# Differential attention in a long kernel: queries and keys of the second heads by seven products of halves, and values and norm of the first heads one step sooner

## The chip, the cores and the metric

One Trainium2 chip, one of its cores. The metric is the time of one execution of the whole program in microseconds (us) on the device; the program before the change takes 1809.34 us (median of three runs, 1808.73 to 1809.43).

## The reference, cut to what matters

The program computes two blocks: a Mamba-2 mixer, a mixture of experts (MoE), a differential attention, a second MoE, and then a second block of two more layers. The change touches the differential attention alone. There x is 256 tokens by 1024 features (in the kernel: xT, features on the partitions), and

```python
q, k, v = split(x @ w_qkv)          # each 256 x 1024; 8 heads, each of two parts of 64
q, k = rope(q), rope(k)             # on 16 of each 64 columns
p1, p2 = softmax(causal(q1 k1^T / 8)), softmax(causal(q2 k2^T / 8))
o = (p1 - lambda * p2) @ v          # per head, 128 wide
o = rms_norm(o) * subln * (1 - lambda_init)
mix = o @ w_o
```

The heads are worked on in two halves ("hg" 0 and 1) of four heads, that is 512 columns of q, k and v each.

## The kernel before, in words

Five in-order instruction streams, one for each engine, are written out by hand; they meet through semaphores (`wait_ge`, `then_inc`). What one function issues on TensorE has its counterparts on ScalarE (copies out of PSUM, exponentials), VectorE (largest scores, shares, rope, norm) and GpSimd (the reciprocal root of the norm, line 3174). `tensor_attention`, `scalar_attention` and `vector_attention` call these parts in a fixed order.

The parts that matter:

- `tensor_qkv(hg, w, t)`: one product of 128 tokens (t) with 512 columns (w: 0 queries, 1 keys, 2 values), eight float32 matmuls 128x512 over the 1024 features. Each float32 matmul stands as two records in the profile, so a product has 16 records (line 212). `scalar_qkv` copies its result (line 1928).
- `tensor_turn_qk` (line 1094) transposes queries or keys after `vector_rope` (lines 2705 to 2711); `scalar_turned_qk` copies them to SBUF (line 1933).
- `tensor_scores(hd)` lays the mask (line 1107) and adds the scores of a head (line 1114). VectorE takes the largest scores (lines 2723, 2725), ScalarE the exponentials (lines 1943, 1945), VectorE the shares (lines 2730 to 2738), and `tensor_turn_p(hd)` transposes them (line 1125), ScalarE copies (line 1950), `tensor_values(hd)` multiplies with the values (lines 1136 to 1138), ScalarE copies and squares (lines 1955 to 1958).
- `vector_subln_var` (line 2786), GpSimd, and `vector_subln` (lines 2791, 2793) do the norm of two heads; `tensor_subln` transposes the result (line 1147), `scalar_subln` copies it (line 1963), and `tensor_attn_out` multiplies with w_o.

Between the scores of a head and the transposition of its shares TensorE is given other work: for the heads 0 to 3 the five products of the second half's queries, keys and values, for head 4 the second half of the product (1, 2, 1), that is the values of the last 128 tokens, and for the heads 5 to 7 pieces of the output projection.

PSUM banks are handed out in turn (`Banks`): who takes a bank waits for what its last user signals. The weights pass through a ring of 8 slots of 2 MB (and a ninth place, xl). `Ring.add` gives each load the slot that has rested longest and the signal that frees it; SyncE issues all loads in order, each after that signal. The first expert weights of the second MoE are loaded while the attention runs. A MoE takes pairs of experts: gate and up products (line 876), down products (line 911), rows gathered (line 810) and spread (line 928).

Of the kernel before, what the change touches and what calls it, by code (L numbers as in the profile page):

```python
# [150 lines left out]
def build(nc, A, out):  # L151
    ctx = ExitStack()
    with ctx:
# [55 lines left out]
        def project(e, bout, lhs, rhs, ks, start=True, stop=True):  # L209
# [62 lines left out]
        QKV = [(0, w, t) for t in range(2) for w in range(3)] + [(1, 2, 0)] + [  # L272
            (1, w, t) for w in range(2) for t in range(2)] + [(1, 2, 1)]
        QKV_LOADS = [(0, 0), (0, 1), (0, 2), (1, 2), (1, 0), (1, 1)]
        qkv_mm, qkv_in = Sig(sem("qkv_mm"), QKV), Sig(sem("qkv_in"), QKV)
        roped = sig("roped", range(2), range(2))
        TQK = [(0, 0), (0, 1), (1, 0), (1, 1)]
# [34 lines left out]
        tu_mm, tu_in = Sig(sem("tu_mm"), TU), Sig(sem("tu_in"), TU)  # L312
        PAIRED = ((0, 0), (1, 0), (0, 1), (1, 1))
        es_mm = Sig(mm_seg.sem, [(u, *x) for u in range(4) for x in PAIRED + ((0, 2),)] + [
            (u, j, t) for u in range(4, 8) for j in range(2) for t in range(2 if j else 3)], mm_seg)
# [17 lines left out]
        oc_in, sq_in, b_in, y_in = then(gained, G8, range(2)), then(xd_in, G8), then(dec_d, G8), then(dec_in, G8)  # L333
        oo_in = Sig(yv_in.sem, [x[0:3] for x in OUT], yv_in)
        og_in, lr_in, lt_in = then(zs_in, G8, range(2)), then(mx_in, G8, G8), then(Bl_in, G8)
        la_in, rt_in, ix_in = then(dec_e, G8), then(S0_in, G8), then(y_rs, G8)


# [54 lines left out]
        ring_moe(0)  # L393
        assert ring.before(*PARTED[:1], 0, *PARTED[1:]) == gate_mm(0, 1, 0)
        for hg, w in QKV_LOADS:
            ring.add(("qkv", hg, w), 1, qkv_mm(hg, w, 1), NSLOT - 1)

        ring.add(("ao", 0), 1, ao_mm(0, 1, 1), NSLOT - 1)
        ring.add(("ao", 1), 1, ao_mm(1, 1, 1), NSLOT - 1)
# [104 lines left out]
        oT = area(big, 0, (8, 256))  # L504
        qT = [area(big, 2048, (4, 256)), area(big, 3072, (4, 256))]
        kT = [area(ring_t[:, NSLOT - 1, :], i * 1024, (4, 256)) for i in range(2)]

        m = Arena(small, 704)
        m(32)
# [562 lines left out]
        def tensor_qkv(e, hg, w, t, ks=range(8)):  # L1072
# [94 lines left out]
        def tensor_attention(e):  # L1167
            for t in range(2):
                if t == 0:
                    tensor_warm(e, row_b[0], 12)  # L1170
                for n in range(2):
                    e.wait_ge(*ln_out("f0", t, n))
                    tensor_turn(e, "f0", t, n, ps[4 * t + n])
                if t == 0:
                    for n in range(2):
                        e.wait_ge(*xT_in("f0", 0, n))
                        tensor_qkv(e, 0, 0, 0, range(4 * n, 4 * n + 4))
            tensor_qkv(e, 0, 1, 0)
            tensor_qkv(e, 0, 2, 0)
            e.wait_ge(*lp_in(0))  # L1180
            e.matmul(ps[7][:, 0:2], ones[:, :], lp, start=True, stop=True).then_inc(*lam_mm.up(0))
            ab.gone[id(ps[7])] = lam_e(0)
            e.wait_ge(*xT_in("f0", 1, 1))
            for w in range(3):
                tensor_qkv(e, 0, w, 1)
            tensor_qkv(e, 1, 2, 0)
            tensor_turn_qk(e, 0, 0)
            tensor_turn_qk(e, 0, 1)
            tensor_scores(e, 0)
            tensor_scores(e, 1)  # L1190
            tensor_qkv(e, 1, 0, 0)
            tensor_turn_p(e, 0)
            tensor_qkv(e, 1, 0, 1)
            tensor_values(e, 0)
            for hd in (1, 2):
                tensor_scores(e, hd + 1)
                tensor_turn_p(e, hd)
                tensor_qkv(e, 1, 1, hd - 1)
                tensor_values(e, hd)
            tensor_turn_p(e, 3)  # L1200
            tensor_qkv(e, 1, 2, 1, range(4))
            tensor_turn_qk(e, 1, 0)
# [24 lines left out]
            tensor_attn_out(e, 1, 1, 1)  # L1227
# [738 lines left out]
        def scalar_attention(e):  # L1966
# [17 lines left out]
            scalar_qkv(e, 1, 2, 0)  # L1984
            scalar_turned_qk(e, 0, 0)
            scalar_turned_qk(e, 0, 1)
            scalar_scores(e, 0)
            scalar_scores(e, 1)
            scalar_qkv(e, 1, 0, 0)
            scalar_turned_p(e, 0)  # L1990
            scalar_qkv(e, 1, 0, 1)
            scalar_values(e, 0)
            for hd in (1, 2):
                scalar_scores(e, hd + 1)
                scalar_turned_p(e, hd)
                scalar_qkv(e, 1, 1, hd - 1)
                scalar_values(e, hd)
            scalar_turned_p(e, 3)
            scalar_turned_qk(e, 1, 0)
            scalar_turned_qk(e, 1, 1)  # L2000
# [695 lines left out]
        def vector_rope(e, hg, w):  # L2696
# [4 lines left out]
            e.wait_ge(*qkv_in(hg, w, 1))  # L2701
            e.wait_ge(*trig(1))
            if hg or w:
                e.wait_ge(*(roped(hg, 0) if w else roped(0, 1)))
# [4 lines left out]
            e.wait_ge(*vs())  # L2709
            e.tensor_tensor(r1, u[0], u[1], ALU.subtract).then_inc(*vs.up())  # L2710
            e.tensor_tensor(r2, u[2], u[3], ALU.add).then_inc(*roped.up(hg, w))

        def vector_scores(e, hd):
            vector_largest_score(e, hd)
# [26 lines left out]
        def vector_attention(e):  # L2741
# [763 lines left out]
```

## Time and profile before

| | |
|---|---|
| median of three runs | 1809.34 us (1808.73 to 1809.43) |
| the profiled execution, its own time | 1808.5 us |
| span of its trace | 1806.7 us |
| TensorE busy | 1785.8 us, 99% |
| VectorE busy | 721.7 us, 40% |
| ScalarE busy | 448.5 us, 25% |
| granted clock of TensorE | 1.00 of full speed |

The span is the time from the first to the last instruction. A share of busy time is an average over stages that have different limits. An engine's idle time costs nothing as long as the engine is not the one that is waited for.

### The profile page before, as it was taken

To read this page: it belongs to the slowest core of one execution; us is meant where nothing else is said; L and a number is where in the kernel's file an instruction comes from. 1 tells how busy PE (TensorE), PEld (TensorE's weight loads), DVE (VectorE), ACT (ScalarE), POOL (GpSimd) and SP (SyncE) were. 2 spreads that over 40 slices of the span, in tenths; PEclk is the share of its full clock that TensorE was granted. 3 is DMA by queue.
4 is the path that set the end of the run, shared out by engine and by line. 5 is a ranking of instruction groups with operands and counts; after the bars stand their busy time and mean duration, and the time that the engine had idled before them with its cause. 6 is when DMAs were issued, how large, how long until landed. Compare 5 with 4: busy or idle time off the path is not lost.

```text
span 1806.7 us, 21260 instructions
## 1 busy us (share of the span) xinstructions
PE 1785.8 (99%) x8612; PEld 983.8 (54%) x8647; DVE 721.7 (40%) x1667; ACT 448.5 (25%) x958; POOL 70.9 (4%) x66
## 2 busy tenths in 40 slices
PE   9999999999999999999999999999999999999999
PEld 8888754443443333455444344343366767568874
DVE  3566754212221213045421221221345566244675
ACT  2332312111111101143211111110134534217780
POOL 0000000000000000000000000000011110001110
PEclk9999999999999999999999999999999999999999
DMA  9723469999999999708999999999932332041520
GB/s 387 306 76 146 186 254 404 426 427 427 427 428 427 427 428 425 315 0 349 359 424 428 427 428 426 428 427 427 425 158 94 140 122 112 7 181 47 238 89 23
DMA packets 41684, 527.41 MB, mean 292 GB/s; under 512 B 4784, under 2 KB 5456, under 8 KB 8560
## 3 DMA queue, kind: packets, MB, share of 16 engines
q1 hardware_dynamic: 39056, 516.70, 68.8%
q10 hardware_dynamic: 2528, 9.31, 1.3%
q8 instruction: 71, 1.16, 0.3%
q14 instruction: 29, 0.24, 0.0%
HBM read 524.91 MB, written 1.08 MB: 291 GB/s over the span
## 4 chain that ended last, share of the span: by engine, by line
PE 87%; DMA 9%; DVE 2%; SPq 1%; issue 0%; ACT 0%; POOL 0%; DVEq 0%; ACTq 0%
PE ps L212 32%; PE ps L876 20%; PE ps L911 10%; DMA ring<-in_wu 6%; PE ps L810 4%; PE ps L928 3%; DMA ring<-in_w_lat 2%; PE ps L715 2%; PE ps L1698 2%; PE ps L1666 2%; PE ps L1234 1%; DMA big<-in_w_z0dt 1%; PE ps L679 1%; PE ps L1713 1%; PE ps L883 1%; PE ps L1446 1%
## 5 line engine op out<-in xcount | busy, mean ns | idle before, releaser
L876 PE MATMUL ps<-ring,work 128*64 128x512 f32 x1856 | 408.9, 593 | 5.5 <-DMA ring<-in_wu 5.1
L212 PE MATMUL ps<-xl,ring 128*128 128x256 f32 (+3 forms) x1344 | 291.6, 375 | 0.6 <-DMA ring<-in_w_x 0.6
L876 PEld LDWEIGHTS ps<-ring,work 128*64 128x64 f32 x1856 | 131.6, 137 | 269.9 <-issue 251.0
L212 PEld LDWEIGHTS ps<-xl,ring 128*128 128x128 f32 x1344 | 243.7, 190 | 39.8 <-issue 2.7
L911 PE MATMUL ps<-ring,work 128*64 128x512 f32 x816 | 181.5, 594 | 0.1
L212 PE MATMUL ps<-ring,xl 128*128 128x256 f32 (+1 forms) x576 | 176.0, 463 | 0.2 <-ACT xl L1783 0.2
L2643 DVE TENSOR_TENSOR work<-work,ps 128x512 f32<-128x512 f32 x32 | 22.0, 687 | 360.6 <-PE ps L876 340.9
L212 PEld LDWEIGHTS ps<-ring,xl 128*128 128x128 f32 x576 | 108.3, 190 | 59.3 <-issue 49.9
L911 PEld LDWEIGHTS ps<-ring,work 128*64 128x64 f32 x816 | 56.2, 137 | 100.3 <-issue 98.7
L3174 POOL TENSOR_TENSOR small<-small,halves 128x1 f32<-128x1 f32 (+4 forms) x42 | 45.7, 1089 | 1546.3 <-DVE small L2445 935.8
L2604 DVE SCALAR_TENSOR_TENSOR work<-ps,small,big 128x512 f32<-128x512 f32 x60 | 45.0, 750 | 135.8 <-ACT big L1914 135.8
L1899 ACT COPY work<-ps 128x512 f32<-128x512 f32 x32 | 18.8, 586 | 305.5 <-PE ps L883 305.5
L1914 ACT ACTIVATE big<-ps,small 128x512 bf16<-128x512 f32 x60 | 41.2, 687 | 182.7 <-PE ps L911 182.7
L212 PE MATMUL ps<-ring,big 128*128 128x512 f32 x192 | 86.2, 595 | 0.2 <-ACT big L1963 0.2
L810 PE MATMUL ps<-work,big 128*128 128x256 bf16 x672 | 78.0, 273 | 0.0
L928 PE MATMUL ps<-big,work 128*128 128x512 bf16 x270 | 69.4, 379 | 4.8 <-issue 4.8
L810 PEld LDWEIGHTS ps<-work,big 128*128 128x128 bf16 x672 | 65.3, 98 | 12.1 <-issue 4.9
L1895 ACT ACTIVATE work<-ps 128x512 f32<-128x512 f32 x32 | 19.1, 597 | 180.8 <-PE ps L876 180.7
L2613 DVE COPY work<-ps 128x512 f32<-128x512 f32 x32 | 22.1, 691 | 97.8 <-PE ps L810 97.1
L212 PEld LDWEIGHTS ps<-ring,big 128*128 128x128 f32 x192 | 34.9, 190 | 39.5 <-issue 39.3
L928 PEld LDWEIGHTS ps<-big,work 128*128 128x128 bf16 x300 | 26.7, 98 | 52.0 <-issue 26.0
L212 PE MATMUL ps<-ring,work 128*128 128x512 f32 (+2 forms) x144 | 50.6, 501 | 0.0
(476 smaller groups left out, 1958.3 us busy)
## 6 DMA issues: line engine op xcount, KB each, us to landing
ring<-in_wg SPq DMA_DIRECT2D x62, 2048.0 KB, 20.2
ring<-in_wu SPq DMA_DIRECT2D x52, 2048.0 KB, 21.4
ring<-in_wd SPq DMA_DIRECT2D x48, 2048.0 KB, 21.9
xl<-in_wd SPq DMA_DIRECT2D x10, 2048.0 KB, 23.2
xl<-in_wu SPq DMA_DIRECT2D x9, 2048.0 KB, 18.4
ring<-in_w_odd SPq DMA_DIRECT2D x8, 2048.0 KB, 7.5
ring<-in_w_xz SPq DMA_DIRECT2D x7, 2048.0 KB, 23.1
ring<-in_w_qkv SPq DMA_DIRECT2D x6, 2048.0 KB, 36.0
```

Of the source, the lines that this page charges most:

```text
L212: i = e.matmul(bout, lhs(k), rhs(k), start=start and k == ks[0], stop=stop and k == ks[-1])
L715: last = e.matmul(oacc[name][:, :], lhs[:, m, :], rhs[:, m, :], start=m == 0 and name in ("p1", "p5", "p2"), stop=m == 6, skip_group_check ...
L810: last = e.matmul(o, hb[:, j, t, c:c + 128], Sb[:, s // 2 % 2, t, :], start=t + j == 0, stop=t + j == 3)
L876: last = e.matmul(b[64 * j:64 * j + 64, :], x[:, 4 * a + k, 64 * j:64 * j + 64], w[k // 2][:, 2 * (k % 2) + j, :], start=a + k == 0, stop= ...
L911: last = e.matmul(b[64 * j:64 * j + 64, :], hT[:, f, 64 * j:64 * j + 64], w[:, j, :], start=f == 0, stop=f == 3)
L928: last = e.matmul(macc[t][n][:, :], SWT[:, p % 2, t * 128:(t + 1) * 128], ypart(j, n), start=p + j == 0, stop=False)
L1666: e.matmul(b[:, c0:272], wl[:, ki, r, (2 * cb + j) % 8, :], xc[cb % 2][:, j, c0:272], start=True, stop=True).then_inc(*lr_mm.up(cb, i))
L1698: last = e.matmul(eb["oo", OB[name]][:, :], lhs[:, k, :], w, start=first and k == 0, stop=k == 5, skip_group_check=True)
L1914: e.activation(ypart(0, n), row_b[n][:, :], ACT.Copy, scale=wsl[:, p % 2:p % 2 + 1]).then_inc(*yh.up(l, p, n))
L2604: e.scalar_tensor_tensor(out=hs, in0=row_b[n][:, :], scalar=wsl[:, p % 2:p % 2 + 1], in1=ypart(0, n), op0=ALU.mult, op1=ALU.subtract).then ...
L2613: e.tensor_copy(gathered(s, 0), gat_b(s)[0][:, :].rearrange("p (k n) -> p k n", k=4 if s < 2 else 2)).then_inc(*xg0.up(l, s))
L3174: e.tensor_tensor(x, x, n[0:x.shape[0]], ALU.pow).then_inc(*done)
```

## The change

Queries and keys of the second half of the heads were four products (two halves of the tokens, queries or keys), each over all features, thirty-two matmuls. They are now computed as a 2 by 2 by 2 block product (token halves, feature halves, queries and keys) with seven products of halves instead of eight: p1 to p7, four matmuls each. For this VectorE forms four sums of x (128x512 each), four sums of the weights (128x2048 each), and ScalarE copies partial results out while VectorE adds others to them. A further ring slot, "qksum", holds the sums. Rope of the second half takes the keys first. The second product of values (1, 2, 1) is finished before the scores of head 4 where its second half came after them; the values of head 3 come before the transpositions of the second half's keys and queries where they came after; and VectorE's norm of the first heads comes ahead of head 4's largest scores.

```diff
-        for hg, w in QKV_LOADS: ring.add(("qkv", hg, w), 1, qkv_mm(hg, w, 1), NSLOT - 1)
+            ring.add(("qkv", hg, w), 1, qkv_mm(hg, w, 1) if hg == 0 or w == 2 else qk_mm("p7" if w else "p4"), NSLOT - 1)
+        ring.add(("qksum",), 0, qk_mm("p7"), NSLOT - 1)
...
+        def tensor_qk_mix(e, name):
+            lhs, rhs = {
+                "p1": (xa(0, 0), wqk(0, 0)), "p5": (xsum[0], qksum), "p2": (xa(0, 1), wqk(1, 0)), "p6": (xsum[1], wqk(0, 0)),
+                "p3": (xsum[3], wqk(1, 1)), "p7": (xsum[2], wqk(0, 1)), "p4": (xa(1, 1), wqk(1, 0))}[name]
...   (waits: p5 on t1; p6 on t2 and r11; p3 on r22; p7 on r12; p4 on t4)
+            for k in range(4):
+                last = e.matmul(ab["qk", bank][:, :], lhs[:, k, :], rhs[:, k, :], start=first and k == 0, stop=k == 3,
+                                skip_group_check=True)
...
@@ tensor_attention
             tensor_qkv(e, 1, 2, 0)
+            tensor_qk_mix(e, "p1")
             tensor_turn_qk(e, 0, 0)
             tensor_turn_qk(e, 0, 1)
             tensor_scores(e, 0)
             tensor_scores(e, 1)
-            tensor_qkv(e, 1, 0, 0)
+            tensor_qk_mix(e, "p5")
+            tensor_qk_mix(e, "p2")
             tensor_turn_p(e, 0)
-            tensor_qkv(e, 1, 0, 1)
+            tensor_qk_mix(e, "p6")
+            tensor_qk_mix(e, "p3")
             tensor_values(e, 0)
-            for hd in (1, 2):
-                tensor_scores(e, hd + 1)
-                tensor_turn_p(e, hd)
-                tensor_qkv(e, 1, 1, hd - 1)
-                tensor_values(e, hd)
+            tensor_scores(e, 2)
+            tensor_turn_p(e, 1)
+            tensor_qk_mix(e, "p7")
+            tensor_qk_mix(e, "p4")
+            tensor_values(e, 1)
+            tensor_scores(e, 3)
+            tensor_turn_p(e, 2)
+            tensor_qkv(e, 1, 2, 1, range(4))
+            tensor_values(e, 2)
             tensor_turn_p(e, 3)
-            tensor_qkv(e, 1, 2, 1, range(4))
+            tensor_qkv(e, 1, 2, 1, range(4, 8))
+            tensor_values(e, 3)
+            tensor_turn_qk(e, 1, 1)
             tensor_turn_qk(e, 1, 0)
-            tensor_turn_qk(e, 1, 1)
-            tensor_values(e, 3)
             tensor_scores(e, 4)
-            tensor_qkv(e, 1, 2, 1, range(4, 8))
             tensor_subln(e, 0, 0)
             tensor_subln(e, 0, 1)
@@ scalar_attention (after the copies for heads 0 to 2, with r11, r22, r12, r21 in them)
             scalar_turned_p(e, 3)
-            scalar_turned_qk(e, 1, 0)
+            scalar_values(e, 3)
+            scalar_qkv(e, 1, 2, 1)
             scalar_turned_qk(e, 1, 1)
-            scalar_values(e, 3)
+            scalar_turned_qk(e, 1, 0)
             scalar_scores(e, 4)
-            scalar_qkv(e, 1, 2, 1)
+        def vector_qk_sums(e):
...   (s1 to s4 of x, then t1 and t3 of the weights, then t2, which waits for p1)
+        def vector_qk_add(e, name, done, copied, bank, x):
+            e.wait_ge(*qk_mm(done))
+            e.wait_ge(*qk_copied(copied))
+            e.tensor_tensor(x, x, ab["qk", bank][:, :], ALU.add).then_inc(*qk_mix.up(name))
@@ vector_attention
             vector_rope(e, 0, 1)
+            vector_qk_sums(e)
             for hd in (0, 1):
                 vector_scores(e, hd)
+            e.wait_ge(*qk_mm("p2"))
+            e.wait_ge(*qk_mix("t2"))
+            e.tensor_tensor(wqk(1, 0), wqk(1, 0), wqk(0, 0), ALU.subtract).then_inc(*qk_mix.up("t4"))
+            vector_qk_add(e, "c11", "p2", "r11", "c", qs[:, 0, :])
             vector_scores(e, 2)
+            vector_qk_add(e, "c12", "p3", "r12", "f", ks_[:, 0, :])
+            vector_qk_add(e, "c22", "p7", "r21", "a", ks_[:, 1, :])
+            vector_rope(e, 1, 1)
+            vector_scores(e, 3)
+            vector_qk_add(e, "c21", "p4", "r21", "e", qs[:, 1, :])
             vector_rope(e, 1, 0)
-            vector_scores(e, 3)
-            vector_rope(e, 1, 1)
             vector_subln_var(e, 0, 0)
             vector_subln_var(e, 0, 1)
-            vector_largest_score(e, 4)
             vector_subln(e, 0, 0)
             vector_subln(e, 0, 1)
+            vector_largest_score(e, 4)
             vector_shares(e, 4)
```

## Rows read from the trace of the kernel before

**Rows 1.** The page: span; busy time of the engine.

```profile
span 1806.7 us, 21260 instructions
PE 1785.8 (99%) x8612; PEld 983.8 (54%) x8647; DVE 721.7 (40%) x1667; ACT 448.5 (25%) x958; POOL 70.9 (4%) x66
```

**Rows 2.** Waits of TensorE, 760 to 852 us: instruction, releaser, us, times, longest.

```profile
PE ps L212 <- ACT big L1963: 0.2, 1, 0.2
```

**Rows 3.** Timeline of TensorE: start, us, line, tiles, records [idle before].

```profile
736.29 27.71 PE L212 MATMUL ps<-ring,xl 128*128 128x512 f32 x64
763.84 1.91 PE L1094 MATMUL ps<-cF,work 128*128 128x128 f32 x16
...
769.01 7.13 PE L212 MATMUL ps<-ring,xl 128*128 128x512 f32 x16
...
802.23 0.49 PE L1125 MATMUL ps<-cF,work 128*128 128x128 f32 x3
802.56 3.60 PE L212 MATMUL ps<-ring,xl 128*128 128x512 f32 x8
806.00 1.91 PE L1094 MATMUL ps<-cF,work 128*128 128x128 f32 x16
807.74 0.39 PE L1136 MATMUL ps<-work 128*128 128x128 f32 x2
...
808.41 0.49 PE L1107 MATMUL ps<-cB 128*128 128x384 bf16 x2
808.83 0.93 PE L1114 MATMUL ps<-ring,big 64*128 64x128 f32 x8
809.69 3.70 PE L212 MATMUL ps<-ring,xl 128*128 128x512 f32 x8
813.23 1.04 PE L1147 MATMUL ps<-cF,work 128*128 128x128 f32 x8
814.10 0.49 PE L1107 MATMUL ps<-cB 128*128 128x384 bf16 x2
...
815.37 0.55 PE L1125 MATMUL ps<-cF,work 128*128 128x128 f32 x3
```

**Rows 4.** Timeline of VectorE.

```profile
767.82 1.15 DVE L2723 TENSOR_REDUCE small<-ps 128x1 f32<-128x128 f32 x4 [15.47 <-PE ps L1114]
...
809.79 1.15 DVE L2723 TENSOR_REDUCE small<-ps 128x1 f32<-128x128 f32 x4
...
814.38 0.48 DVE L2738 SCALAR_TENSOR_TENSOR work<-work,small 128x256 f32<-128x256 f32 x1
```

**Rows 5.** Timeline of ScalarE.

```profile
806.63 1.07 ACT L1933 COPY big<-ps 128x512 f32<-128x512 f32 x2 [2.78 <-PE ps L1094]
807.59 1.09 ACT L1933 COPY ring<-ps 128x512 f32<-128x512 f32 x2
808.61 0.37 ACT L1955 COPY work<-ps 128x256 f32<-128x256 f32 x1
```

**Rows 6.** Groups by line and form on VectorE: count, us in all, mean ns.

```profile
L2671 DVE TENSOR_TENSOR work<-h,big 128x2048 f32<-128x2048 f32 x2 | 4.6, 2284 | 0.0
```

**Rows 7.** SyncE's queue: landing of the loads of in_w_qkv, then issues by start.

```profile
DMA to landing us min/median/max: 31.8/36.0/44.4
...
708.04 0.33 SPq L3232 DMA_DIRECT2D ring<-in_w_qkv  x1
...
757.16 56.58 SPq L3232 DMA_DIRECT2D ring<-in_wu  x2
...
851.06 0.33 SPq L3232 DMA_DIRECT2D ring<-in_wd  x1
```

**Rows 8.** Windows: stretch, length, busy PE, PEld, DVE, ACT, POOL, clock, DMA, GB/s.

```profile
790.00:810.00 20.00, 20.00 (x91) 11.45 (x90) 6.49 (x28) 8.67 (x31) 1.08 (x2) 1.00 0.00 1
840.00:850.00 10.00, 10.00 (x27) 4.62 (x26) 6.23 (x12) 0.69 (x1) 0.99 (x1) 1.00 0.70 298
1300.00:1304.00 4.00, 2.56 (x19) 0.47 (x17) 2.86 (x5) 1.39 (x4) 0.54 (x1) 1.00 1.01 426
```

More of the change, by code:

```diff
@@ L271, in build @@
         lp_in, lam_mm, lam_e = (sig(n, range(1)) for n in ("lp_in", "lam_mm", "lam_e"))
-        QKV = [(0, w, t) for t in range(2) for w in range(3)] + [(1, 2, 0)] + [
-            (1, w, t) for w in range(2) for t in range(2)] + [(1, 2, 1)]
+        QKV = [(0, w, t) for t in range(2) for w in range(3)] + [(1, 2, 0), (1, 2, 1)]
+        qk_mm = then(mm_seg, ("p1", "p5", "p2", "p6", "p3", "p7", "p4"))
+        qk_copied = then(zs_in, ("r11", "r22", "r12", "r21"))
+        qk_mix = then(xd_in, ("s1", "s2", "s3", "s4", "t1", "t3", "t2", "t4", "c11", "c12", "c22", "c21"))
         QKV_LOADS = [(0, 0), (0, 1), (0, 2), (1, 2), (1, 0), (1, 1)]
         qkv_mm, qkv_in = Sig(sem("qkv_mm"), QKV), Sig(sem("qkv_in"), QKV)
-        roped = sig("roped", range(2), range(2))
-        TQK = [(0, 0), (0, 1), (1, 0), (1, 1)]
+        TQK = [(0, 0), (0, 1), (1, 1), (1, 0)]
+        roped = Sig(sem("roped"), TQK)
         qkT_mm = Sig(sem("qkT_mm"), [k + (i,) for k in TQK for i in range(2)])
@@ L314, in build @@
         es_mm = Sig(mm_seg.sem, [(u, *x) for u in range(4) for x in PAIRED + ((0, 2),)] + [
-            (u, j, t) for u in range(4, 8) for j in range(2) for t in range(2 if j else 3)], mm_seg)
+            (u, j, t) for u in range(4, 8) for j in range(2) for t in range(2 if j else 3)], qk_mm)
         es_exp = then(nega_e, U8, range(2), range(3))
@@ L332, in build @@
         odd_mix = then(mix, ("t1a", "t1", "t3", "s1", "s3", "r11", "s2", "t2", "r22", "s4", "t4", "r12", "r21", "r2b"))
-        oc_in, sq_in, b_in, y_in = then(gained, G8, range(2)), then(xd_in, G8), then(dec_d, G8), then(dec_in, G8)
+        oc_in, sq_in, b_in, y_in = then(gained, G8, range(2)), then(qk_mix, G8), then(dec_d, G8), then(dec_in, G8)
         oo_in = Sig(yv_in.sem, [x[0:3] for x in OUT], yv_in)
-        og_in, lr_in, lt_in = then(zs_in, G8, range(2)), then(mx_in, G8, G8), then(Bl_in, G8)
+        og_in, lr_in, lt_in = then(qk_copied, G8, range(2)), then(mx_in, G8, G8), then(Bl_in, G8)
         la_in, rt_in, ix_in = then(dec_e, G8), then(S0_in, G8), then(y_rs, G8)
@@ L395, in build @@
         for hg, w in QKV_LOADS:
-            ring.add(("qkv", hg, w), 1, qkv_mm(hg, w, 1), NSLOT - 1)
+            ring.add(("qkv", hg, w), 1, qkv_mm(hg, w, 1) if hg == 0 or w == 2 else qk_mm("p7" if w else "p4"), NSLOT - 1)
+        ring.add(("qksum",), 0, qk_mm("p7"), NSLOT - 1)
         ring.add(("ao", 0), 1, ao_mm(0, 1, 1), NSLOT - 1)
@@ L506, in build, with xa, wqk @@
         kT = [area(ring_t[:, NSLOT - 1, :], i * 1024, (4, 256)) for i in range(2)]
+        xsum = [area(ring.view("qksum"), 512 * i, (4, 128)) for i in range(4)]
+        qksum = area(ring.view("qksum"), 2048, (4, 512))
+        def xa(t, hf):
+            return xT[:, hf:8:2, t * 128:(t + 1) * 128]
+        def wqk(hf, n):
+            return kview(8, 512)(ring.view("qkv", 1, n))[:, hf:8:2, :]
         m = Arena(small, 704)
@@ L1083, in tensor_qkv @@
                 last.then_inc(*qkv_mm.up(hg, w, t))
+        def tensor_qk_mix(e, name):
+            lhs, rhs = {
+                "p1": (xa(0, 0), wqk(0, 0)), "p5": (xsum[0], qksum), "p2": (xa(0, 1), wqk(1, 0)), "p6": (xsum[1], wqk(0, 0)),
+                "p3": (xsum[3], wqk(1, 1)), "p7": (xsum[2], wqk(0, 1)), "p4": (xa(1, 1), wqk(1, 0))}[name]
+            bank = {"p1": "a", "p6": "a", "p7": "a", "p5": "f", "p3": "f", "p2": "c", "p4": "e"}[name]
+            first = name in ("p1", "p5", "p2", "p4")
+            if first:
+                last_read = {"f": "c12", "c": "c11", "e": "c21"}
+                b, gone = ab.hold(("qk", "a")) if bank == "a" else ab.take(("qk", bank), qk_mix(last_read[bank]))
+                if gone:
+                    e.wait_ge(*gone)
+            if name == "p1":
+                e.wait_ge(*ring("qkv", 1, 0))
+            elif name == "p5":
+                e.wait_ge(*qk_mix("t1"))
+            elif name == "p6":
+                e.wait_ge(*qk_mix("t2"))
+                e.wait_ge(*qk_copied("r11"))
+            elif name == "p3":
+                e.wait_ge(*qk_copied("r22"))
+            elif name == "p7":
+                e.wait_ge(*qk_copied("r12"))
+            elif name == "p4":
+                e.wait_ge(*qk_mix("t4"))
+            for k in range(4):
+                last = e.matmul(ab["qk", bank][:, :], lhs[:, k, :], rhs[:, k, :], start=first and k == 0, stop=k == 3,
+                                skip_group_check=True)
+            last.then_inc(*qk_mm.up(name))
+            if name == "p7":
+                ab.give(ab["qk", "a"], qk_mix("c22"))
         def tensor_turn_qk(e, hg, w):
@@ L1928, in scalar_qkv, with scalar_qk_copy @@
             e.copy((qs, ks_, vs_[hg])[w][:, t, :], ab["qkv", hg, w, t][:, :]).then_inc(*qkv_in.up(hg, w, t))
+        def scalar_qk_copy(e, name, done, bank, to):
+            e.wait_ge(*qk_mm(done))
+            e.copy(to, ab["qk", bank][:, :]).then_inc(*qk_copied.up(name))
         def scalar_turned_qk(e, hg, w):
@@ L1986, in scalar_attention @@
             scalar_turned_qk(e, 0, 1)
+            scalar_qk_copy(e, "r11", "p1", "a", qs[:, 0, :])
             scalar_scores(e, 0)
             scalar_scores(e, 1)
-            scalar_qkv(e, 1, 0, 0)
+            scalar_qk_copy(e, "r22", "p5", "f", ks_[:, 1, :])
             scalar_turned_p(e, 0)
-            scalar_qkv(e, 1, 0, 1)
+            scalar_qk_copy(e, "r12", "p6", "a", ks_[:, 0, :])
             scalar_values(e, 0)
[L1993 to L1997, printed above, removed]
+            scalar_scores(e, 2)
+            scalar_turned_p(e, 1)
+            scalar_qk_copy(e, "r21", "p7", "a", qs[:, 1, :])
+            scalar_values(e, 1)
+            scalar_scores(e, 3)
+            scalar_turned_p(e, 2)
+            scalar_values(e, 2)
             scalar_turned_p(e, 3)
+            scalar_values(e, 3)
+            scalar_qkv(e, 1, 2, 1)
+            scalar_turned_qk(e, 1, 1)
             scalar_turned_qk(e, 1, 0)
-            scalar_turned_qk(e, 1, 1)
-            scalar_values(e, 3)
             scalar_scores(e, 4)
-            scalar_qkv(e, 1, 2, 1)
             scalar_subln(e, 0, 0)
@@ L2700, in vector_rope @@
             u = [x.rearrange("p t (c d) -> p t c d", c=8) for x in u4]
-            e.wait_ge(*qkv_in(hg, w, 1))
+            if hg:
+                e.wait_ge(*qk_mix("c22" if w else "c21"))
+            else:
+                e.wait_ge(*qkv_in(hg, w, 1))
             e.wait_ge(*trig(1))
             if hg or w:
-                e.wait_ge(*(roped(hg, 0) if w else roped(0, 1)))
+                e.wait_ge(*((roped(0, 1) if w else roped(1, 1)) if hg else roped(0, 0)))
             e.tensor_tensor(u[0], r1, cb_, ALU.mult).then_inc(*vs.up())
@@ L2711, in vector_rope @@
             e.tensor_tensor(r2, u[2], u[3], ALU.add).then_inc(*roped.up(hg, w))
+        def vector_qk_sums(e):
+            e.wait_ge(*xT_in("f0", 1, 1))
+            e.wait_ge(*ring.before("qksum"))
+            e.tensor_tensor(xsum[0], xa(1, 0), xa(1, 1), ALU.add).then_inc(*qk_mix.up("s1"))
+            e.wait_ge(*qk_mix("s1"))
+            e.tensor_tensor(xsum[1], xsum[0], xa(0, 0), ALU.subtract).then_inc(*qk_mix.up("s2"))
+            e.tensor_tensor(xsum[2], xa(0, 0), xa(1, 0), ALU.subtract).then_inc(*qk_mix.up("s3"))
+            e.wait_ge(*qk_mix("s2"))
+            e.tensor_tensor(xsum[3], xa(0, 1), xsum[1], ALU.subtract).then_inc(*qk_mix.up("s4"))
+            e.wait_ge(*ring("qkv", 1, 0))
+            e.wait_ge(*ring("qkv", 1, 1))
+            e.tensor_tensor(qksum, wqk(0, 1), wqk(0, 0), ALU.subtract).then_inc(*qk_mix.up("t1"))
+            e.wait_ge(*qk_mix("t1"))
+            e.tensor_tensor(wqk(0, 1), wqk(1, 1), wqk(0, 1), ALU.subtract).then_inc(*qk_mix.up("t3"))
+            e.wait_ge(*qk_mix("t3"))
+            e.wait_ge(*qk_mm("p1"))
+            e.tensor_tensor(wqk(0, 0), wqk(0, 1), wqk(0, 0), ALU.add).then_inc(*qk_mix.up("t2"))
+        def vector_qk_add(e, name, done, copied, bank, x):
+            e.wait_ge(*qk_mm(done))
+            e.wait_ge(*qk_copied(copied))
+            e.tensor_tensor(x, x, ab["qk", bank][:, :], ALU.add).then_inc(*qk_mix.up(name))
         def vector_scores(e, hd):
@@ L2761, in vector_attention @@
             vector_rope(e, 0, 1)
+            vector_qk_sums(e)
             for hd in (0, 1):
                 vector_scores(e, hd)
+            e.wait_ge(*qk_mm("p2"))
+            e.wait_ge(*qk_mix("t2"))
+            e.tensor_tensor(wqk(1, 0), wqk(1, 0), wqk(0, 0), ALU.subtract).then_inc(*qk_mix.up("t4"))
+            vector_qk_add(e, "c11", "p2", "r11", "c", qs[:, 0, :])
             vector_scores(e, 2)
+            vector_qk_add(e, "c12", "p3", "r12", "f", ks_[:, 0, :])
[3 more added lines that the diff above has]
+            vector_qk_add(e, "c21", "p4", "r21", "e", qs[:, 1, :])
             vector_rope(e, 1, 0)
-            vector_scores(e, 3)
-            vector_rope(e, 1, 1)
             vector_subln_var(e, 0, 0)
             vector_subln_var(e, 0, 1)
-            vector_largest_score(e, 4)
             vector_subln(e, 0, 0)
             vector_subln(e, 0, 1)
+            vector_largest_score(e, 4)
             vector_shares(e, 4)
```

## The prediction

> **What bounds the kernel now.** I read the page first: TensorE is busy 1785.8 us of a span of 1806.7 [rows 1]. Then its waits in the attention: between 760 and 852 us it waits 0.2 us in all [rows 2]. So in this stretch every microsecond taken from TensorE's list comes off the end, and every microsecond for which its next instruction is not ready is added. Therefore the third view, the timeline of TensorE there [rows 3], together with those of VectorE and ScalarE [rows 4, 5]: each result that TensorE uses is made by a chain through those two, and what counts is how much work TensorE has in hand meanwhile. Last, the DMA side [rows 7, 8], since the second MoE behind the attention is fed from it.
>
> **Lengths of TensorE's pieces**, from start to start [rows 3]: four products take 763.84 - 736.29 = 27.55 us, so 6.89 each; a half product (four matmuls, 8 records) 806.00 - 802.56 = 3.44; both turns of queries and keys 807.74 - 806.00 = 1.74; values of a head 808.41 - 807.74 = 0.67; mask 0.42, scores 0.86 (808.41, 808.83, 809.69), 1.28 together; a turn of shares 802.56 - 802.23 = 0.33; two norm turns 814.10 - 813.23 = 0.87.
>
> **What is removed.** Four products of 16 records (64) become seven of 8 (56): 8 records, 3.44 us less. The seven are matmuls of the same form, reading operands of the same width.
>
> **The sums on VectorE.** s1 to s4 are 128x512, about 0.7 us each, t1 and t3 are 128x2048, 2.28 us each by the row of that width [rows 6]: 7.4 us, and VectorE stands idle 15.47 us there, until 767.82 [rows 4]. Both weights are used later before than now, but they landed some 15 us before VectorE comes to them, at about 755 (the last one is issued at 708.04 and lands after 31.8 us, or 44.4 if it were the slowest of the six) [rows 7]. t2 waits for p1, which ends at 763.84 + 3.44 = 767.28, and is done at 769.8; head 0's scores stand behind the turns and end 3.44 later than before, 771.2. So t2 is hidden; were it half as long again it would end at 770.7, still before them, and head 0's shares are wanted only at 779.3, when 771.2 and the chain below make 776.5. t4 and the four additions (0.7 each, 5 us in all) lie in VectorE's gaps between heads. Cost of all this: zero, from both ends. The ScalarE copies r11, r22, r12, r21 replace four of the same size. The waits of p5, p6, p3, p7, p4 on these all come out as met, the tightest of them with over 2 us.
>
> **The chain of a head.** From the end of its scores to the turn of its shares: VectorE starts 0.10 us after TensorE has moved on (809.69 to 809.79), the chain largest, exponentials, shares takes 814.38 + 0.48 - 809.79 = 5.07 us [rows 4]; the signal to TensorE I take as 0.15, as ScalarE's copy ends at 807.59 + 1.09 = 808.68 and the scores that wait for it start at 808.83 [rows 3, 5] (ends 0.05 and 0.3). Together 5.32 us. TensorE must have that much work in hand.
>
> **Lay the new order on these numbers.** Head 1's scores end at 769.01 + 3.44 = 772.45. p5, p2 to 779.33, turn 0 779.66, p6, p3 to 786.54, values 0 787.21, scores 2 to 788.49, turn 1 788.84, p7, p4 to 795.72, values 1 796.39, scores 3 to 797.67. No wait so far.
>
> First wait: turn 3. Behind scores 3 now stand turn 2 (0.35), half a product (3.44) and values 2 (0.67) = 4.46 us, where before a whole product stood. 5.32 - 4.46 = 0.86 us of waiting. Turn 3 then is at 802.99, with its half product and values 3 to 807.43.
>
> Second wait: scores 4. The turns of keys and queries end at 809.17, the mask (a bank that ScalarE frees late costs 0.14) at 809.73. But ScalarE has put the values of head 3 ahead of them: it starts these at 807.63 and needs about 0.96, then 0.48 for the product's copy, then four copies of 0.48 (806.63 to 807.59 for two, 1.09 until the last has ended) [rows 5]; the last turned quarter is there at 807.63 + 0.96 + 0.48 + 3 x 0.48 + 0.61 = 811.12, at TensorE 811.27. Wait 1.54; with the bank 1.68. Before, the copies of the turns stood ahead of the values (807.59 ahead of 808.61) and TensorE did values 3 in between. Scores 4 end at 812.13.
>
> Third wait, the largest: turn 4. Before, half a product (813.23 - 809.69 = 3.54), the norm turns and scores 5 stood behind scores 4, 815.37 - 809.69 = 5.68 us, 0.4 more than the chain needs. The half product is now ahead; 0.87 + 1.28 = 2.15 us are left. 5.32 - 2.15 = 3.17 us of waiting. Turn 4 is at 817.45 against 815.37: 2.1 later. That the norm stands sooner on VectorE brings nothing against this: the norm's turns come before scores 5 in both orders and are ready (807.43 + 0.2 + 1.05 for the squares, 1.3 for GpSimd, 0.9 for the scaling: 810.9, before scores 4 end).
>
> The sum: -3.44 + 0.86 + 1.68 + 3.17 = +2.3 by pieces, +2.1 by the clock of the timeline (the difference is the switching of the pieces that I rounded). I take +2.2 us. After turn 4 the order is unchanged; head 5's shares are ready with 0.8 us to spare, and TensorE had no slack there to take anything back [rows 2]. The ends: with 0.05 or 0.3 us for the signal the sum is +1.9 or +2.6; if each half product costs the 3.54 of the other row instead of 3.44, +0.7 more.
>
> **The clock of TensorE.** It stands at 1.00, the 2.4 GHz level, in every window, in the emptiest one too (2.56 us busy of 4) [rows 8]. The trace has no idle stretch as long as 3.17 us, so it does not say what follows one. The Trainium skill, TensorE: Matmul & The Clock Gate, Part 1, says that the gate passes half the pulses after TensorE was idle and releases it with sustained activity; by the row the sum is +2.2, by that rule it would be that of the first rival below.
>
> **The DMA side.** Now "qksum" takes the slot that a load had, so each later load moves on by one: the two loads of attn_out wait for the first half's queries and keys, done by 736.29 + 2 x 6.89 = 750.1, and the load of the first up weights (issued at 757.16 before) joins the one that waits for the product (1, 2, 1), 757.16 + 56.58 = 813.7 before [rows 7], 806.8 now. Four loads of 2 MB instead of three start there, 4.9 us each at 426 GB/s [rows 8], until 826.5; next in line are three that wait for scores 7, 2 us later than before, until about 841, and one that waits for the output products, until about 846. The DMA engines are idle from 790 to 810 and only 0.70 busy from 840 to 850 [rows 8], so the queue is empty before the load that waits for the last output product (851.06) [rows 7] in both kernels. From there on each load of the MoE waits for the same event as before, only in another slot: the MoE with its DMA queue begins 2.2 us later and is otherwise the same. Cost zero; nothing absorbs the 2.2 either.
>
> **To the median.** The profiled execution took 1808.5 us, 0.84 below the median. Its time becomes 1808.5 + 2.2 = 1810.7, the median 1809.34 + 2.2 = 1811.5 us. A measurement of this kernel tells apart about 0.2%, 3.6 us; this is 0.12%, so it would read as no change.
>
> **The rivals.**
> A, the other side: slower by over 0.2%. The idle stretch of 3.17 us at turn 4 (with 1.54 some 4 us ahead of it) lets the granted clock fall to the 1.2 GHz level, and what follows runs at half speed for a while. Price: turn 4, a half product's length of output projection and values 4 are 0.33 + 3.44 + 0.67 = 4.4 us of work [rows 3]; at half speed 4.4 more, so +6.6 in all, 1815.9. It decides once more than 1.4 us of work run at that level. For it: such a hole is nowhere in the trace. Against it: clock 1.00 everywhere, also with 2.56 of 4 us busy. Chance 0.11.
> B: the waits are mostly covered, because the chain of a head or the copies run faster when ScalarE and VectorE have little else; then -3.44 with perhaps the first wait, 1806 to 1807. Against it: the 5.07 us are one engine's work after the other's, and VectorE was free when head 4's chain began. Chance 0.06.
> C: the later start of the MoE is absorbed, as its last loads bound it anyhow. Price 0 to +0.5, 1809.5. For it: the DMA engines are full to the end of the MoE (1.01 at 1300) [rows 8]. Against it: the last loads ahead of the MoE wait for TensorE (851.06) [rows 7]. Chance 0.06.
> D: the burst of four loads is late for the first pairs of experts; each load is 4.9 us, so +7 and 1816.5. It needs a burst that lasts until 851; I have it end 5 to 10 us ahead. Chance 0.03.
>
> **How the numbers follow.** My forecast has 0.74 and its own range is 1811.0 to 1812.6; within the 0.2% it holds nearly whole. Faster by over 0.2% (below 1805.7) is the far end of B only: 0.02. Slower by over 0.2% (above 1813.0) is A, D and a part of the switching costs: 0.15. No change 0.83. The range that holds 8 in 10 is 1809.4 to 1814.0.
>
> **What would show it.** In the trace after: TensorE waits at line 1125 (turns of shares) twice, 0.9 and 3.2 us, released by VectorE's line of the last share, and once at line 1114 (scores), 1.5 us, released by ScalarE's copy of turned queries; 8 records less on line 212; VectorE idle still at 760; t2 done before head 0's scores. I am wrong if TensorE waits at any of p5 to p4, if the clock stands below 1.00 at 817, or if the second MoE shows longer waits on DMA than before.

## The result, and the profile after

The changed kernel takes 1811.91 us (median of 22 runs, 1809.53 to 1814.11), the kernel before 1808.43 us (22 runs beside them): ratio 1.0018, 95% interval 1.0012 to 1.0024, that is 2.2 to 4.3 us more. The forecast was +2.2 us, a time of 1811.5 us and no change to within 0.2%. The medians differ by 3.5 us, just inside that 0.2%. The profiled execution took 1814.11 us, the slowest of its 22, so its span is not the typical one. Its span is 5.6 us longer than that of before (1812.3 against 1806.7): 1.3 us of this lie ahead of the attention, 3.6 in it and 0.7 behind it.

The waits of TensorE between 755 and 860 us (instruction, releaser, us in total, times, longest), where before there was one of 0.2 us [rows 2]:

```profile
PE ps L1169 <- DVE work L2822: 3.5, 2, 3.0
PE ps L1158 <- ACT big L1987: 1.4, 1, 1.4
PE ps L212 <- ACT big L2017: 0.2, 1, 0.2
```

Line 1169 turns shares (1125 before), 1158 are scores (1114), 2822 is the last step of the shares, 1987 the copy of turned queries or keys. These are the three waits of the forecast, at the instructions and from the releasers that it named. The timeline of TensorE (start, us, line, tiles, records [idle before]), answering to [rows 3]:

```profile
737.62 27.71 PE L212 MATMUL ps<-ring,xl 128*128 128x512 f32 x64
765.17 3.60 PE L1123 MATMUL ps<-ring,xl 128*128 128x512 f32 x8
768.60 1.91 PE L1138 MATMUL ps<-cF,work 128*128 128x128 f32 x16
...
773.77 3.70 PE L1123 MATMUL ps<-ring 128*128 128x512 f32 x8
...
804.31 0.55 PE L1169 MATMUL ps<-cF,work 128*128 128x128 f32 x3 [0.58 <-DVE work L2822]
804.69 3.60 PE L212 MATMUL ps<-ring,xl 128*128 128x512 f32 x8
...
812.52 0.93 PE L1158 MATMUL ps<-ring,big 64*128 64x128 f32 x8 [1.44 <-ACT big L1987]
813.38 1.09 PE L1191 MATMUL ps<-cF,work 128*128 128x128 f32 x8
...
818.61 0.55 PE L1169 MATMUL ps<-cF,work 128*128 128x128 f32 x3 [2.96 <-DVE work L2822]
818.99 5.30 PE L212 MATMUL ps<-ring,big 128*128 128x512 f32 x8
824.13 0.38 PE L1180 MATMUL ps<-work 128*128 128x128 f32 x2
...
855.80 1.04 PE L593 MATMUL ps<-cF,h 128*128 128x128 f32 x8
```

This execution comes to the attention 1.33 us later than the one of before (737.62 against 736.29), so lengths are to be compared, not times. From that row to head 4's turned shares it is 80.99 us against 79.08 [rows 3]: 1.9 more. The row behind it is the one that the forecast did not have: eight records of the output projection take 5.30 us instead of 3.60. The windows (length, then busy PE, PEld, DVE, ACT, POOL, granted clock, share and GB/s of DMA) show why:

```profile
812.00:816.00 4.00, 3.13 (x26) 2.07 (x26) 1.60 (x6) 1.60 (x7) 0.00 (x0) 1.00 0.96 410
816.00:820.00 4.00, 1.39 (x5) 0.88 (x6) 3.03 (x11) 2.37 (x8) 0.00 (x0) 0.89 1.05 451
820.00:824.00 4.00, 4.00 (x7) 1.62 (x7) 1.79 (x6) 1.57 (x8) 0.00 (x0) 0.69 0.98 422
824.00:828.00 4.00, 4.00 (x24) 2.43 (x23) 1.32 (x5) 1.94 (x9) 0.00 (x0) 1.00 1.02 432
```

The granted clock stood at 1.00 until the idle stretch of 2.96 us, and fell behind it: 0.69 on the mean of 4 us is a part of them at the 1.2 GHz level (in one experiment below a whole window reads 0.50). The Trainium skill, TensorE: Matmul & The Clock Gate, Part 1, has the gate halve the clock after TensorE was idle and release it with activity; this trace agrees in kind, 5.30 us for 3.60. So the clock fell as in rival A, for less than half the price set there (1.7 us, not 4.4) and on top of the forecast. The prediction had named a clock below 1.00 at 817 us as a sign of being wrong, and it reads 0.89 there.

To the end of the attention (line 593, 581 before) it is 118.18 us against 850.87 - 736.29 = 114.58: +3.60. That is 1.9 up to the turned shares and 1.7 in the slower row behind them. This length is the measure for the experiments below; it leaves out what executions differ by elsewhere.

VectorE, answering to [rows 4]:

```profile
758.45 2.29 DVE L2787 TENSOR_TENSOR ring<-ring 128x2048 f32<-128x2048 f32 x1
768.88 2.29 DVE L2790 TENSOR_TENSOR ring<-ring 128x2048 f32<-128x2048 f32 x1 [8.13 <-PE ps L1123]
772.59 1.15 DVE L2807 TENSOR_REDUCE small<-ps 128x1 f32<-128x128 f32 x4 [1.42 <-PE ps L1158]
...
813.48 1.15 DVE L2807 TENSOR_REDUCE small<-ps 128x1 f32<-128x128 f32 x4 [1.21 <-PE ps L1158]
...
818.07 0.48 DVE L2822 SCALAR_TENSOR_TENSOR work<-work,small 128x256 f32<-128x256 f32 x1
```

t3 is done at 760.74, t2 waits 8.1 us for p1 and is done 1.4 us before head 0's scores: hidden, as laid out. Head 4's chain is again 818.07 + 0.48 - 813.48 = 5.07 us. ScalarE, answering to [rows 5]:

```profile
809.00 0.37 ACT L2009 COPY work<-ps 128x256 f32<-128x256 f32 x1 [3.62 <-PE ps L1182]
...
809.95 0.58 ACT L1978 COPY work<-ps 128x512 f32<-128x512 f32 x1
810.42 1.08 ACT L1987 COPY ring<-ps 128x512 f32<-128x512 f32 x2
811.37 1.10 ACT L1987 COPY big<-ps 128x512 f32<-128x512 f32 x2
```

Values of head 3, the product's copy, then the turned keys and queries: the last ends at 812.47, and scores 4 start at 812.52, 0.05 us later.

The DMA issues of SyncE, answering to [rows 7]:

```profile
758.50 0.33 SPq L3324 DMA_DIRECT2D ring<-in_wg  x1
808.32 0.81 SPq L3324 DMA_DIRECT2D ring<-in_wu  x2
809.18 0.43 SPq L3324 DMA_DIRECT2D ring<-in_wd  x1
809.66 22.64 SPq L3324 DMA_DIRECT2D ring<-in_wg  x2
856.00 0.33 SPq L3324 DMA_DIRECT2D ring<-in_wd  x1
```

The burst starts at 808.3, 5.4 us ahead of before (6.8 counted from the start of the attention; the forecast had 6.9), and the load at 856.00 waits for the last output product as the one at 851.06 did. In the second MoE TensorE waits 2.5 us on `in_wu` in both kernels. At the end of it there is one wait on DMA, for `in_w_lat`, that was shorter before (1.44 us, here 2.29):

```profile
1302.12 1.91 PE L1234 MATMUL ps<-ring,mzT 128*16 128x512 f32 x16 [1.44 <-DMA ring<-in_w_lat]
```

Of the traces below, two with the same further ring slot have 1.09 and 1.56 us there (e1, e2), and the one without the seven products has 2.26 (e3). So one trace of each does not tie this wait to the change.

### The profile page after: what moved, and what is told of

It reads as the page before. It is cut to its first block, busy times and chain, and to the rows that moved or that the text cites. A ratio compares the mean times of both kernels' runs of the same rounds, so it can differ in the third digit from the quotient of the medians.

```text
span 1812.3 us, 21266 instructions
## 1 busy us (share of the span) xinstructions
PE 1785.6 (99%) x8604; PEld 983.9 (54%) x8639; DVE 736.1 (41%) x1679; ACT 448.1 (25%) x958; POOL 70.9 (4%) x66
## 4 chain that ended last, share of the span: by engine, by line
PE 86%; DMA 9%; DVE 2%; ACT 1%; SPq 1%; issue 0%; POOL 0%; DVEq 0%; ACTq 0%
PE ps L212 30%; PE ps L888 20%; PE ps L923 10%; DMA ring<-in_wu 6%; PE ps L822 4%; PE ps L940 3%; DMA ring<-in_w_lat 2%; PE ps L727 2%; PE ps L1748 2%; PE ps L1716 2%; PE ps L1123 1%; PE ps L1284 1%; DMA big<-in_w_z0dt 1%; PE ps L691 1%; PE ps L1763 1%; PE ps L895 1%
## 5 line engine op out<-in xcount | busy, mean ns | idle before, releaser
L212 PE MATMUL ps<-ring,xl 128*128 128x256 f32 (+1 forms) x512 | 147.7, 446 | 0.2 <-ACT xl L1833 0.2
L212 PEld LDWEIGHTS ps<-ring,xl 128*128 128x128 f32 x512 | 96.5, 190 | 45.2 <-issue 35.8
```

Of the source, the lines that this page charges most:

```text
L212: i = e.matmul(bout, lhs(k), rhs(k), start=start and k == ks[0], stop=stop and k == ks[-1])
```

## The experiments

Each was timed beside the kernel before. The changed kernel did not run among them, so it is compared with them through the kernel before: +3.5 us in its own 22 runs. "Length" is that of the attention stretch in the one profiled execution of each (114.58 before, 118.18 changed).

**Filling the third wait (e2).** The edit, on the changed kernel:

```diff
         def tensor_turn_p(e, hd):
-            e.wait_ge(*p_in(hd))
             b, gone = ab.take(("pT", hd), pT_in(hd))
             if gone:
                 e.wait_ge(*gone)
+            if hd == 4:
+                tensor_warm(e, b, 12)
+            e.wait_ge(*p_in(hd))
```

> The changed kernel, and ahead of the wait for head 4's shares TensorE multiplies 12 bf16 matmuls of 128x512 into the bank that the turn takes next (0.22 us each, 2.6 us in all; their result is overwritten). My theory: the wait of 2.96 us stays as time, but TensorE is busy in it, the clock stays at 1.00 (0.89 and 0.69 between 816 and 824 us in the changed kernel), the half product's length of output projection behind it takes 3.60 us instead of 5.30, and the kernel is 1.7 us faster than the changed one: about +2 us against the kernel before. Rival: the fall of the clock is no cause but chance of the one profile, or the clock was going to fall anyway from the three waits together; then +3.5 us as the changed kernel.

Measured: 1810.17 us (before beside it 1808.45), ratio 1.0009 (1.0000 to 1.0018), +1.7 us; length 116.58, +2.0. The timeline of TensorE:

```profile
814.66 2.54 PE L589 MATMUL ps<-cB 128*128 128x512 bf16 x11 [0.16 <-issue]
817.46 0.55 PE L1171 MATMUL ps<-cF,work 128*128 128x128 f32 x3 [0.27 <-DVE work L2824]
817.85 3.60 PE L212 MATMUL ps<-ring,big 128*128 128x512 f32 x8
```

(The profile has 11 records of the 12. The edit asks for the bank ahead of the shares at every turn, and the first wait is 0.68 us here for 0.58.) The chain is not a bit shorter, yet the kernel is faster: 3.60 us again behind it, and +2.0 is close to the forecast's +2.2. The intervals of the two times overlap (here 0.0 to 3.3 us, 2.2 to 4.3 for the changed kernel); what bears the reading out is the row behind the wait and the mean clock, 1.000 in all 11 runs here and in 5 of 22 there. So the clock is a term of its own, 1.7 us in this place.

**Filling less of it (e7).** The same with `tensor_warm(e, b, 5)`.

> The changed kernel with 5 instead of 12 idle-filling matmuls (1.1 us) ahead of the wait for head 4's shares, so that some 1.8 us of idle time are left there. If the clock falls only after a stretch as long as the whole wait, it stays at 1.00 and the kernel is as the one with 12: +1.7 to +2 us against the kernel before. Rival: also this stretch lets it fall, as 2.3 us did in the kernel before with the half product ahead: +3.3 to +3.6.

Measured: 1810.10 us (before 1808.10), ratio 1.0010 (1.0001 to 1.0019), +2.0 us; length 116.55. A stretch of 1.77 us without work did not let the clock fall here:

```profile
817.21 0.55 PE L1171 MATMUL ps<-cF,work 128*128 128x128 f32 x3 [1.77 <-DVE work L2824]
817.59 3.60 PE L212 MATMUL ps<-ring,big 128*128 128x512 f32 x8
```

**The half product behind the scores again (e1)**, the seven products kept:

```diff
             tensor_turn_p(e, 3)
-            tensor_qkv(e, 1, 2, 1, range(4, 8))
             tensor_values(e, 3)
             tensor_turn_qk(e, 1, 1)
             tensor_turn_qk(e, 1, 0)
+            ab.skip(1)
             tensor_scores(e, 4)
+            tensor_qkv(e, 1, 2, 1, range(4, 8))
...   ScalarE: scalar_qkv(e, 1, 2, 1) behind scalar_scores(e, 4)
...   VectorE: vector_largest_score(e, 4) ahead of the two vector_subln
```

> The changed kernel with the second half of product (1, 2, 1) behind head 4's scores again, its copy behind head 4's exponentials, head 4's largest scores ahead of the norm, and one bank skipped ahead of the scores (without that the scores would wait for the bank that this product holds). My theory: the third wait is gone (5.6 us of work behind the scores against a chain of 5.3), and with it the fall of the clock; the first wait (0.6) stays, values 3 now waits 0.8 for its turned shares, scores 4 about 1.2 for the copies: -0.6 us against the kernel before. Rival: the waits come from the seven products (their sums on VectorE, the ring slot, the later loads) and not from where the half product stands; then this stays near +3.

Measured: 1807.67 us (before 1808.45), ratio 0.9996 (0.9987 to 1.0005), -0.8 us; length 113.86, -0.7. Its waits:

```profile
PE ps L1158 <- ACT big L1988: 1.0, 1, 1.0
PE ps L1180 <- DVE work L2796: 0.6, 1, 0.6
PE ps L1169 <- DVE work L2823: 0.6, 1, 0.6
```

The profile puts the wait of line 1180 down to VectorE, but the values wait for ScalarE's copy of the turned shares, which ends at 804.53, and they start at 804.62. Both waits ahead of head 4 came 0.2 us shorter than expected (0.6 for 0.8, 1.0 for 1.2). There is no wait at head 4's shares, and the kernel takes 4.3 us less than the changed one with the same seven products, by the times (-0.8 for +3.5) and by the lengths. Against the kernel before, the -0.8 is not clear of the noise (-2.4 to +0.9). The one skipped bank matters: the half-finished product holds a PSUM bank, and with the banks in their plain turn scores 4 take just this one and never start. That is argued from the order in which banks are taken; it was not run.

**The half product ahead of the scores, without the seven products (e3).** On the kernel before:

```diff
             tensor_values(e, 3)
+            tensor_qkv(e, 1, 2, 1, range(4, 8))
             tensor_scores(e, 4)
-            tensor_qkv(e, 1, 2, 1, range(4, 8))
...   ScalarE: scalar_qkv(e, 1, 2, 1) ahead of scalar_scores(e, 4)
```

> The kernel before, without the seven products, with one thing moved: the second half of product (1, 2, 1) stands ahead of head 4's scores on TensorE, and its copy ahead of head 4's exponentials on ScalarE. My theory: the move alone opens the waits; by laying the order on the durations, 2.4 us at the norm's turn of heads 0 and 1, 0.4 at the next and 0.4 at head 4's shares, +3.1 us in all, and the clock may fall or not. Rival: the order is without effect and the seven products are the cause: 0.

Measured: 1812.83 us (before 1808.45), ratio 1.0024 (1.0015 to 1.0033), +4.4 us; length 118.51, +3.9: 2.3 us of idle time and 1.6 us of slower matmuls behind it:

```profile
816.21 1.94 PE L1147 MATMUL ps<-cF,work 128*128 128x128 f32 x8 [2.32 <-DVE work L2793]
817.94 0.85 PE L1107 MATMUL ps<-cB 128*128 128x384 bf16 x2
818.72 1.34 PE L1114 MATMUL ps<-ring,big 64*128 64x128 f32 x8
819.99 0.55 PE L1125 MATMUL ps<-cF,work 128*128 128x128 f32 x3
```

The same three pieces took 815.37 - 813.23 = 2.14 us before [rows 3], here 3.78. The two waits of 0.4 that I expected behind the first did not come; that the slower pieces cover them is argued, not shown. This move alone costs as much as the whole change does (+4.4 and +3.5, with intervals that overlap).

**The norm behind the largest scores (e6).** On the changed kernel, VectorE only:

```diff
-            vector_subln(e, 0, 0)
-            vector_subln(e, 0, 1)
             vector_largest_score(e, 4)
+            vector_subln(e, 0, 0)
+            vector_subln(e, 0, 1)
```

> The changed kernel with VectorE's order of before at one place: head 4's largest scores ahead of the norm of heads 0 to 3. My theory: nothing is won or lost by this step of the change, since the norm's results then come late instead of head 4's shares: waits of about 2.4 and 0.4 us at the norm's turns and 0.4 at head 4's shares in place of 3.0 us at the shares. With the clock falling as in the kernel before with the half product ahead: +3.5 us against the kernel before, as the changed kernel. Rival: the norm standing sooner is what costs (it delays the largest scores of head 4); then this is faster than the changed kernel by up to 1.6 us.

Measured: 1811.85 us (before 1808.10), ratio 1.0020 (1.0011 to 1.0029), +3.7 us, as the changed kernel; length 118.57. Its waits, 2.3 us at the norm's turn in place of 3.0 at the shares, none at the shares of head 4 (the 0.6 below are head 3's):

```profile
PE ps L1191 <- DVE work L2885: 2.3, 1, 2.3
PE ps L1158 <- ACT big L1987: 1.4, 1, 1.4
PE ps L1169 <- DVE work L2822: 0.6, 1, 0.6
```

The waits are 0.6 us shorter than in the changed kernel, but the clock takes more: a whole window reads 0.50, and from the norm's turn (814.82) to values 4 (823.54) it is 8.7 us where 6.0 are usual, 2.7 us more instead of 1.7.

```profile
816.00:820.00 4.00, 4.00 (x18) 2.61 (x17) 2.48 (x9) 1.47 (x3) 0.00 (x0) 0.50 0.98 418
```

So with the half product ahead of the scores, the norm one step sooner neither costs nor brings anything that the times show.

**The copies first (e4).** On the changed kernel, ScalarE only:

```diff
             scalar_turned_p(e, 3)
-            scalar_values(e, 3)
             scalar_qkv(e, 1, 2, 1)
             scalar_turned_qk(e, 1, 1)
             scalar_turned_qk(e, 1, 0)
+            scalar_values(e, 3)
             scalar_scores(e, 4)
```

> The changed kernel with ScalarE's copies of the product (1, 2, 1) and of the turned keys and queries ahead of its values of head 3. My theory by the durations: the wait at scores 4 shrinks from 1.4 to 0.6 us, but the norm then starts 2.4 us later, so waits of 1.1 and 0.7 us appear at its turns, and head 4's shares, behind the norm on VectorE, still wait 3.3: +3.2 us in waits and work against the kernel before (the changed kernel +2.1), and 1.7 for the clock on top, +4.9. Rival: the copies' order is the whole second wait and nothing is late behind it; then about 1 us faster than the changed kernel, +2.5.

Measured: 1813.78 us (before 1808.10), ratio 1.0029 (1.0018 to 1.0040), +5.7 us; length 120.38, +5.8. Its waits:

```profile
PE ps L1169 <- DVE work L2822: 3.7, 2, 3.1
PE ps L1191 <- DVE work L2885: 1.7, 2, 1.1
PE ps L1158 <- ACT big L1987: 0.5, 1, 0.5
```

The second wait shrank as expected and came back at the norm and at head 4's shares, which wait for the norm on VectorE. So this order on ScalarE does not buy off the second wait. The clock's part is larger than the 1.7 us that I had set:

```profile
819.11 0.90 PE L1169 MATMUL ps<-cF,work 128*128 128x128 f32 x3 [3.09 <-DVE work L2822]
819.80 6.07 PE L212 MATMUL ps<-ring,big 128*128 128x512 f32 x8
825.72 0.38 PE L1180 MATMUL ps<-work 128*128 128x128 f32 x2
```

Turn and half product take 825.72 - 819.11 = 6.6 us where 3.8 are usual: 2.8 us. The rest of the +5.8, waits and work, is +3.0 for an expected +3.2.

**Every chain covered (e5).** The seven products kept:

```diff
             tensor_qkv(e, 1, 2, 1, range(4))
             tensor_values(e, 2)
+            tensor_turn_qk(e, 1, 1)
             tensor_turn_p(e, 3)
-            tensor_qkv(e, 1, 2, 1, range(4, 8))
+            tensor_turn_qk(e, 1, 0)
             tensor_values(e, 3)
-            tensor_turn_qk(e, 1, 1)
-            tensor_turn_qk(e, 1, 0)
+            ab.skip(1)
             tensor_scores(e, 4)
+            tensor_qkv(e, 1, 2, 1, range(4, 8))
...   ScalarE in the same order; VectorE:
-            vector_scores(e, 3)
+            vector_largest_score(e, 3)
             vector_qk_add(e, "c21", "p4", "r21", "e", qs[:, 1, :])
             vector_rope(e, 1, 0)
+            vector_shares(e, 3)
...   vector_largest_score(e, 4) ahead of the two vector_subln
```

> The seven products kept, the order around them laid so that each chain of shares has as much work behind its scores as it takes: behind scores 3 the turns 2, half a product, values 2 and the turn of the keys; then shares 3, the turn of the queries, values 3, scores 4, the other half of the product. VectorE adds c21 and ropes the queries between head 3's largest scores and its shares, and takes head 4's largest scores ahead of the norm; one bank is skipped ahead of scores 4. My theory: waits of 0.2 and 0.5 us are left, the clock stays, -2.8 us against the kernel before (3.44 less work). Rival (seven products bring nothing whatever the order): 0 or slower.

Measured: 1805.37 us (before 1808.45), ratio 0.9985 (0.9976 to 0.9994), -3.1 us, and the fastest of all; length 847.42 - 735.59 = 111.83, -2.75. Of its waits one is new:

```profile
PE ps L1180 <- ACT work L2005: 0.4, 1, 0.4
```

I had expected waits of 0.2 and 0.5 us. So the 3.44 us of the seven products are real, and most of them come out when next to nothing waits. This order without the seven products was not run; but the kernel before waits 0.2 us in the attention [rows 2], so an order alone had little to win there.

## Why the prediction was right, point by point

The waits were forecast at their places, from their causes and nearly in their sizes. The clock was not in the sum, and that the time of 1811.5 us came within 0.4 of the median is partly luck.

- The work removed: 8 records, 3.44 us. Right; e5 brings 2.75 to 3.1 of it.
- The sums on VectorE cost nothing: right, 2.29 us for each wide one, and no wait at p5 to p4.
- The three waits: expected 0.86, 1.54 with 0.14 for the bank, 3.17; measured 0.58, 1.44, 2.96. Counted from start to start, as the forecast's pieces were, the first is 0.74, the second 1.52 with 0.04 for the bank, the third 3.02; the profile counts idle time from the modelled end of the last matmul and so has a little less. The step that was too long is the signal: I took 0.15 us from an order in which TensorE had not waited for that copy (the row at 808.83 has no idle time before it, [rows 3]). Here the shares end at 818.55 and turn 4 starts at 818.61, 0.06 us later, and from the end of head 4's scores to its turn it is 818.61 - 813.38 = 5.23 us, not 5.32. That gives the +1.9 which the prediction had named as its low end, and +1.9 is what the length up to turn 4 shows.
- The cause, where the half product stands: shown from both sides, by e1 (put back, 4.3 us won) and e3 (moved alone, 4.4 us lost). This holds for the third wait, the largest. The second, which comes from the values of head 3 standing ahead of the turns, is supported by ScalarE's rows and by e4; moving the values alone on TensorE was not run.
- Ring slot and DMA: nothing that the runs show. The waits on `in_wu` are as before. The wait for `in_w_lat` is 0.85 us longer, which by its words is another of the prediction's signs of being wrong; across the kernels it does not follow the change, as said above.
- The other rivals. B: head 4's chain took 5.07 us again and the waits came. C: nothing was taken back, the stretch behind the attention is 0.7 us longer in these two traces. D: no added wait at the first pairs of experts.
- What was not in the sum: the clock. This is the step that failed. I left it at zero because it stood at 1.00 in every window of before, and had its fall as rival A with a chance of 0.11; it fell in every profiled kernel that had an idle stretch of 2.3 us or more in the attention (changed, e3, e4, e6) and, in the attention, in none of the others. The mean clock of the whole run says the same over all runs: 1.000 in all 11 of e1, of e2 and of e5 and in 10 of e7's 11, but in 2 of e3's 11 and in none of e4's 8 and e6's 11. (As an estimate, a mean of 0.999 over 1809 us is 1.8 us of full speed lost.) In the 22 runs of the changed kernel the mean clock is 1.000 in five, and these take 1809.5 to 1810.9, +2.1 us on the average, which is the sum of the forecast; the other seventeen, at 0.998 or 0.999, take 1810.7 to 1814.1. The time of 1811.5 was near the median for a sum that is 1.3 us short, by luck: the median of before was also 0.9 lower in these 22 runs than in the three shown. What the third wait costs is 3.0 us and, in most runs, some 1.7 behind it.

## What to carry to other kernels

Where one engine is busy without a gap, count for every chain through the others how long it is (here 5.2 us from scores to turned shares) and how much work stands behind its start; a piece of work moved from behind the start to ahead of it costs what the chain then lacks in cover, and less work in the cover is no gain. Saved work is worth its time only if the pieces left are laid out anew: the same seven products gave +3.5, -0.8 and -3.1 us in three orders. And an idle stretch of a few us on TensorE is to be priced with the slower matmuls behind it, here 1.6 to 2.8 us.

## What the runs showed that I had not expected

- The clock fell behind idle stretches as short as 2.3 us (e3, e6). That cost 1.6 us more at the matmuls behind it in e3 and 2.7 in e6. It did not fall behind 1.77 us (e7), nor behind the 1.44 of the second wait (changed, e2, e6, e7). The length of one stretch alone does not set what the fall costs: in e6 the windows of 4 us from 812 to 824 read 0.72, 0.50 and 0.92, while e3, with an idle stretch as long, has 0.57 in one window and 1.00 in the next.
- The same fall comes and goes at another place that no edit touched: where TensorE waits for `in_w_lat` at the end of the second MoE. In e7 the wait was 2.29 us, as in the changed kernel, but the rows behind it took nearly twice their time:

```profile
1304.60 3.49 PE L1286 MATMUL ps<-ring,mzT 128*16 128x512 f32 x16 [2.29 <-DMA ring<-in_w_lat]
```

against this in the changed kernel:

```profile
1307.76 1.91 PE L1284 MATMUL ps<-ring,mzT 128*16 128x512 f32 x16 [2.29 <-DMA ring<-in_w_lat]
```

Six of the nine traces have a wait of 2.1 to 2.3 us there. In three of them the row behind it is slow (e3 3.35, e4 3.52, e7 3.49 us), in three it is not (changed, e5, e6: 1.91 us). So the same instructions behind nearly the same wait have both outcomes. That one program has both from run to run is likely from the mean clocks of the changed kernel, and would be a part of the scatter of its times (4.6 us, against 1.9 in e1 and 2.0 in e5); no two traces of one program show it. What decides between the outcomes stays open.
